# Retrieval step of an encoder layer: picks of two heads side by side, rank keys in pairs, two one-hot parts on ScalarE, 40 side rows for 48, new tables

## The reference

```python
q = (h @ wq).reshape(nb, L, 8, 256)
s1 = einsum(q[..., :128], keys1); s2 = einsum(q[..., 128:], keys2)   # 128 scores each
v1, i1 = top_k(s1, 16);  v2, i2 = top_k(s2, 16)
cand = v1[..., :, None] + v2[..., None, :]                          # 256 sums
sc, ci = top_k(cand, 16)
e = i1[ci // 16] * 128 + i2[ci % 16]                                # expert's number
w = softmax(sc)
act = gelu(einsum('td,tjd->tj', h, u_tab[e]))                       # 128 experts a token
y = einsum('tj,tjd->td', w * act, v_tab[e])
```

## Time and profile before

| what | value |
|---|---|
| median of 3 runs | 3218.49 us (3216.95 to 3223.83) |
| the profiled execution | 3227.11 us, its span 3225.4 us |
| PE, DVE, POOL, ACT busy | 91%, 73%, 38%, 22% of the span |
| bytes moved | 919.78 MB, of which gathers 536.94 MB |
| step 6, from its tile 2 to the last row | 1117.7 to 3160 us of the span |

### The profile page before, as it was taken

The page is one execution under the profiler, slowest core; times in us unless marked ns, Lnnn a source line. Parts: engine busy times, 40 slices in busy tenths (PEclk is TensorE's granted clock), DMA queues, the critical chain, the costliest instruction groups (busy, mean ns, idle before and its releaser), DMA issues. The chain is left out here.

```text
span 3225.4 us, 31301 instructions
## 1 busy us (share of the span) xinstructions
PE 2929.4 (91%) x10332; PEld 1580.0 (49%) x10332; DVE 2348.0 (73%) x4427; ACT 701.4 (22%) x1179; POOL 1222.1 (38%) x1101
## 2 busy tenths in 40 slices
PE   6999699779689997899999998997799999999995
PEld 2557477667574443444544553443344444444442
DVE  4696545550688699999999998774766666676775
ACT  3111434321221101343452442342000000000003
POOL 0111111021225545334334335553655444455660
PEclk8998899889889998999999999998899999999997
DMA  4441101023238999899899899999999999999994
GB/s 181 174 163 47 59 27 33 27 79 124 78 98 346 413 387 341 307 327 372 320 334 354 307 348 379 385 415 405 390 405 404 404 404 404 404 403 404 397 395 162
DMA packets 285835, 919.78 MB, mean 285 GB/s; under 512 B 25840, under 2 KB 75248, under 8 KB 278256
## 3 DMA queue, kind: packets, MB, share of 16 engines
q0 software_dynamic: 147456, 536.94, 43.2%
q1 hardware_dynamic: 99584, 301.75, 25.0%
q10 hardware_dynamic: 38640, 79.18, 6.5%
HBM read 830.21 MB, written 87.56 MB: 285 GB/s over the span
## 5 line engine op out<-in xcount | busy, mean ns | idle before, releaser
L1519 PE MATMUL s_pu<-s_hn,s_ut 128*128 128x512 f32 x2304 | 1016.6, 597 | 14.5 <-ACT s_gst L1631 8.0
L1474 POOL DMA_INDIRECT s_slot<-in_u,s_row x512 | 513.9, 1004 | 688.7 <-DVE s_slot L1888 570.8
L1901 DVE SCALAR_TENSOR_TENSOR s_hB<-s_slot,s_dot,s_hB 128x1024 f32<-128x1024 f32 x461 | 585.1, 1284 | 259.8 <-DMA s_slot<-in_v,s_row 225.6
L1474 POOL DMA_INDIRECT s_slot<-in_v,s_row x512 | 561.7, 1097 | 454.8 <-DVE s_hB L1901 369.6
L1519 PEld LDWEIGHTS s_pu<-s_hn,s_ut 128*128 128x128 f32 x2304 | 436.9, 192 | 546.8 <-issue 546.8
L1888 DVE SCALAR_TENSOR_TENSOR s_slot<-s_slot,s_ph 128x1024 f32<-128x1024 f32 x512 | 608.5, 1220 | 64.9 <-DMA s_slot<-in_u,s_row 40.5
L302 PE MATMUL s_ps<-hn_hi,w_hi 128*128 128x512 f32 x704 | 289.1, 411 | 81.9 <-PEq L276 40.7
L1605 PE MATMUL s_pw<-s_ct,s_vt 128*128 128x512 f32 x512 | 243.3, 598 | 45.4 <-DVE s_ct L1909 42.3
L303 PE MATMUL s_ps<-hn_lo,w_hi 128*128 128x512 f32 x704 | 280.6, 399 | 0.0
L1605 PE MATMUL s_pu<-s_ct,s_vt 128*128 128x512 f32 x512 | 242.6, 596 | 0.0
L1605 PE MATMUL s_py<-s_ct,s_vt 128*128 128x512 f32 x512 | 240.6, 592 | 0.0
(11 more groups left out here) (284 smaller groups left out, 3006.6 us busy)
## 6 DMA issues: line engine op xcount, KB each, us to landing
s_ut<-in_u_tiles SPq DMA_DIRECT2D x128, 512.0 KB
s_vt<-in_v_tiles SPq DMA_DIRECT2D x32, 2048.0 KB
s_g<-s_gst ACTq DMA_DIRECT2D x128, 256.0 KB
s_w<-s_wb ACTq DMA_DIRECT2D x16, 2048.0 KB
s_gr<-s_g SPq DMA_DIRECT2D x64, 512.0 KB
s_wr<-s_w SPq DMA_DIRECT2D x16, 2048.0 KB, 35.0
s_ada<-in_ada SPq DMA_DIRECT2D x48, 512.0 KB, 5.3
s_ada<-in_ada SPq DMA_DIRECT2D x4, 2048.0 KB, 24.6
```

The lines of the kernel that those rows point to most:

```text
L1474: pool.indirect_dma_start(out=slot[s][:, :], out_offset=None, in_=io[kind], in_offset=bass.IndirectOffsetOnAxis(ap=row[b][:, j:j + 1], axi ...
L1519: mm = pe.matmul(pu[:, n % 2, :], ut[n % UR][:, k, :], hn[:, k, :], start=(k == 0), stop=(k == DC - 1))
L1901: dve.scalar_tensor_tensor(y, s, dot[b][:, j:j + 1], y, ALU.mult, ALU.add).then_inc(taken, 1)
```

## The change

- Picks: `pick_step` does two heads side by side in 6 steps, each followed by one drain or two, in place of 3 parts a head. There are still 24 steps to a ranking. In step 5 the two lanes are the two blocks.
- `ranked_key`: the array `eq` has the pairs innermost (`[16, 64, 2]` walked in twos, the keys doubled), and the sum over 16 is four adds that halve it in place of one reduction.
- One-hot parts: VectorE makes one part, ScalarE two (16 activations a batch; they and `later_ready` take the place of the third part and its semaphore).
- `SIDE_ROWS` 48 becomes 40, over 74 tiles in place of 98, so that the last is at tile 98. `take_y` moves to tile 100.
- Tables: `RANKED`, `RANK_TILES` 16 to 17, `HOT_AT` and `HOT_TILES`, `sparse_by`; the order of v rows (`wanted`): six rounds without block 3 first, and each v row waits for the row before it of the same block.

```diff
-                for i in range(MADE_PICKS):
-                    for part in range(3):
-                        m.picks[i].part(dve, h, part, sc[:, :, RANKED[i], :])
+                for step in range(PICK_STEPS):
+                    pick_step(dve, [(m.picks[i], h, 0, sc[:, :, RANKED[i], :]) for i in range(MADE_PICKS)], step)
...
+def pick_step(dve, lanes, step):
+
+    if step == 0:
+        for pk, h, v, sc in lanes:
+            for n in range(2):
+                dve.max(out=pk.val[:, 2 * h + n, 0:8], in_=sc[:, n, :])
...
+    elif step == 4:
+        for pk, h, v, sc in lanes:
+            dve.max(out=pk.best[:, h, 0:8], in_=pk.cand[v][:, :])
         dve.drain()
...
-RANKED = (0, 1, 4, 5, 2, 6, 3, 7)
+RANKED = (0, 1, 4, 2, 5, 6, 3, 7)
...
-SIDE_ROWS = 48
+SIDE_ROWS = 40
...
+V_LEAD = 6
 SPARSE_OPS = 2 * SPARSE * P - SIDE_ROWS
-RANK_AT, RANK_TILES = 2, 16
-HOT_AT = (21, 47, 73, 101)
-HOT_TILES = 22
-SIDE_AT, SIDE_TILES = 26, 98
+RANK_AT, RANK_TILES = 2, 17
+HOT_AT, HOT_TILES = (24, 55, 80, 106), (26, 22, 22, 16)
+SIDE_AT, SIDE_TILES = 26, 74
...
-        tenths += (45 if t < RANK_AT else 44 if t < HOT_AT[0] else
-                   29 if t < RANK_AT + RANK_TILES * (len(RANKED) - MADE_PICKS) else 48 if t < 123 else 60)
+        tenths += 45 if t < RANK_AT else 42 if t < 22 else 32 if t < 104 else 43 if t < 123 else 50
...
-            def third_parts(a, r):
+            def later_parts(a, r):
...
-                for i in range(8):
-                    q, t = divmod(i, 2)
-                    o = act.activation(hotw[n % 2][2][:, q, :, t], hot1[n % 2][:, q, :, t], ACT.Copy,
-                                       scale=rest[:, 1, 8 * r + i:8 * r + i + 1])
-                o.then_inc(third_ready, 1)
+                for x in range(2):
+                    for i in range(8):
+                        q, t = divmod(i, 2)
+                        o = act.activation(hotw[n % 2][1 + x][:, q, :, t], hot1[n % 2][:, q, :, t], ACT.Copy,
+                                           scale=rest[:, x, 8 * r + i:8 * r + i + 1])
+                o.then_inc(later_ready, 1)
...
-            take_y()
+                if n == side_tile(SIDE_ROWS - 1) + 2:
+                    take_y()
...
-                    dve.tensor_tensor(eq[:, :, :], halff[s][:, :].unsqueeze(2).broadcast_to([P, P, TOPK]),
-                                      count[:, :].unsqueeze(1).broadcast_to([P, P, TOPK]), ALU.is_equal)
+                    dve.tensor_tensor(eq[:, :, :].rearrange("p a (q t) -> p a q t", t=2),
+                                      halff[s][:, :].rearrange("p (q t) -> p q t", t=2).unsqueeze(1).broadcast_to(shape),
+                                      count[:, :, :].unsqueeze(2).broadcast_to(shape), ALU.is_equal)
...
-                    dve.tensor_reduce(pair_of(i)[:, s, :], eq[:, :, :], AX.X, ALU.add)
+                    for n in (8, 4, 2):
+                        dve.tensor_tensor(eq[:, 0:n, :], eq[:, 0:n, :], eq[:, n:2 * n, :], ALU.add)
+                        dve.drain()
+                    dve.tensor_tensor(pair_of(i)[:, s, :], eq[:, 0, :], eq[:, 1, :], ALU.add)
...
-                for x in range(2):
-                    dve.tensor_tensor(hotw[n % 2][x][:, :, :, :], hot1[n % 2][:, :, :, :], spread(wT[x]), ALU.mult)
+                dve.tensor_tensor(hotw[n % 2][0][:, :, :, :], hot1[n % 2][:, :, :, :], spread(wT[0]), ALU.mult)
...
-                    dve.wait_ge(taken, i - 2)
+                    if j > (0 if b else SIDE_ROWS):
+                        dve.wait_ge(taken, number["v", b, j - 1] + 1)
```

More of the change, by code:

```diff
@@ L1205, in __init__ @@
         self.place = buffer("place", [P, PH, TOPK], U32)
[L1207 to L1214, removed]
+PICK_STEPS = 6
+def pick_step(dve, lanes, step):
[3 more added lines that the diff above has]
+                dve.max(out=pk.val[:, 2 * h + n, 0:8], in_=sc[:, n, :])
+    elif step == 1:
+        for pk, h, v, sc in lanes:
+            for n in range(2):
+                best = pk.val[:, 2 * h + n, 0:8]
+                dve.max_index(pk.key[:, 2 * h + n, 0:8], best, sc[:, n, :])
+                dve.match_replace(out=pk.rep[v][n][:, :], in_to_replace=best, in_values=sc[:, n, :], imm_value=LOWEST)
+    elif step == 2:
+        for pk, h, v, sc in lanes:
+            for n in range(2):
+                dve.max(out=pk.val[:, 2 * h + n, 8:16], in_=pk.rep[v][n][:, :])
+    elif step == 3:
+        for pk, h, v, sc in lanes:
+            for n in range(2):
+                dve.max_index(pk.key[:, 2 * h + n, 8:16], pk.val[:, 2 * h + n, 8:16], pk.rep[v][n][:, :])
+            at = 0
+            for a0, a1, nb in CAND_RANGES:
+                na = a1 - a0
+                dve.tensor_tensor(pk.cand[v][:, at:at + na * nb].rearrange("p (a b) -> p a b", a=na),
+                                  pk.val[:, 2 * h, a0:a1].unsqueeze(2).broadcast_to([P, na, nb]),
+                                  pk.val[:, 2 * h + 1, 0:nb].unsqueeze(1).broadcast_to([P, na, nb]), ALU.add)
+                at += na * nb
+    elif step == 4:
+        for pk, h, v, sc in lanes:
+            dve.max(out=pk.best[:, h, 0:8], in_=pk.cand[v][:, :])
@@ L1215, in best8 @@
         dve.drain()
-        for n in (2 * h, 2 * h + 1):
-            dve.max_index(self.key[:, n, 0:8], self.val[:, n, 0:8], sc[:, n % 2, :])
-            dve.match_replace(out=self.rep[n % 2][:, :], in_to_replace=self.val[:, n, 0:8], in_values=sc[:, n % 2, :],
+        for pk, h, v, sc in lanes:
+            dve.max_index(pk.place[:, h, 0:8], pk.best[:, h, 0:8], pk.cand[v][:, :])
+            dve.match_replace(out=pk.cand2[v][:, :], in_to_replace=pk.best[:, h, 0:8], in_values=pk.cand[v][:, :],
@@ L1219, in best8 @@
                               imm_value=LOWEST)
+    else:
+        for pk, h, v, sc in lanes:
+            dve.max(out=pk.best[:, h, 8:16], in_=pk.cand2[v][:, :])
         dve.drain()
[L1222 to L1249, removed]
+        for pk, h, v, sc in lanes:
+            dve.max_index(pk.place[:, h, 8:16], pk.best[:, h, 8:16], pk.cand2[v][:, :])
@@ L1824, in ranking @@
                         dve.wait_ge(sc_in[i % 2], 16 * ((i - MADE_PICKS) // 2 + 1))
-                    m.picks[i % MADE_PICKS].part(dve, x // 3, x % 3, sc[i % 2][:, x // 3 * 2:x // 3 * 2 + 2, :])
+                    pair, step = divmod(x, PICK_STEPS)
+                    pick_step(dve, [(m.picks[i % MADE_PICKS], h, h % 2, sc[i % 2][:, 2 * h:2 * h + 2, :])
+                                    for h in (2 * pair, 2 * pair + 1)], step)
                 elif x == 24:
@@ L1850, in take_picks @@
                 dve.drain()
+                dve.tensor_copy(rest[:, 0, :], wT[1][:, :])
+                dve.drain()
             def one_hots(a, r):
@@ L2039, in encoder_layer @@
     m.head = head_inputs(m)
-    m.picks = [Picks(m, R0 + 104 * KB + 4608 * s, s) for s in range(MADE_PICKS)]
+    m.picks = [Picks(m, R0 + 104 * KB + 6144 * s, s) for s in range(MADE_PICKS)]
     m.h1_back = m.at("h1_back", [P, DC, T], F32, F0)
```

49 lines of the change are left out of this document (29 added, 20 removed).

## The result

The changed kernel takes 3166.1 us (median of 4 runs, 3162.1 to 3173.8) where the kernel before takes 3218.0 in runs beside it: ratio 0.9838, 95% interval 0.9815 to 0.9861. A second set of runs gave 0.9845 (0.9829 to 0.9862). The forecast was 3177, range 3152 to 3207, faster. The profiled execution took 3162.1 us, its span is 3160.4.

What follows compares the result with a forecast made beforehand. TensorE was taken to bound tiles 27 to 97, transfers everything from tile 98. Terms -23.1 + 2.8 + 5 - 30 + 5 - 1.3 = -41.6 from 3227.1 give 3185.5, less 8.6 for the median: 3177 us, range 3152 to 3207.

Steps and rivals of the forecast that it cites:

- Tile 27: Step 6, start of tile 27: VectorE's shorter work lets TensorE start it at 1313.9, not 1337.0: -23.1 us.
- Tiles 27 to 97: Step 6's middle stretch: TensorE sets the pace, 628.2 us for 625.4, plus 5 for late side rows.
- +2.8: Tiles 27 to 97: two batches fewer and three side rows more on TensorE cost 2.8 us.
- +5: Tiles 27 to 97: side rows that land late, with the gathers' share at 360 GB/s, cost 5 us.
- From tile 98 on: Tile 98 to the last row: transfers bound, 467.2 MB left at 400 GB/s, -30 us, and +5 for tiles 98 to 103.
- The copy of py: `take_y` at tile 100 removes a 32.97 us VectorE stall, priced at nothing because transfers ran at 400 GB/s.
- Step 5, -1.3: Step 5: the last head's picks of two blocks save 8 drains, -1.3 us.
- What would show it: Signs in step 6's trace, among them tile 27 near 1314, tile 98 near 1947, VectorE's v-phase lead used up.
- The stretch's limit: Rival: transfers in tiles 27 to 97 are already at their limit, 337 GB/s; +28 us, 3205; chance 0.14.
- TensorE alone: Rival: TensorE is the bound after tile 98 too, gathers filling every gap; -91 us, 3127; chance 0.04.
- ScalarE: Rival: ScalarE's activations, above 0.37 us each, hold TensorE in each batch's tile; +90 us, 3267; chance 0.05.
- Nothing: Rival: the change changes nothing, as transfers set all of step 6 and its bytes are the same; chance 0.04.

Runs made afterwards that it cites:

- e3: The changed kernel with the copy of py (`take_y`) put back behind the last gelu: 3166.9 us, ratio 0.9800 to the kernel before.
- e5: The changed kernel with gathered v rows from the start of the v phase on fetched at half width: 3138.1 us, ratio 0.9740 to the kernel before.
- e12: The changed kernel with u rows 81 to 174 fetched at half width: 3169.8 us, ratio 0.9803 to the kernel before.
- e1: The changed kernel's new instructions under the tables of the kernel before, with 48 side rows: 3192.7 us, ratio 0.9881 to the kernel before.
- e2: The instructions of the kernel before under the changed kernel's tables, 40 side rows and v-row order: 3200.5 us, ratio 0.9910 to the kernel before.
- e8: The changed kernel with a ranking over 16 tiles; 3.8 rows a tile to tile 23, 3.5 to 81, 3.7 to 103: 3143.2 us, ratio 0.9761.
- e13: The changed kernel with a ranking over 16 tiles; 3.2 rows a tile to tile 23, 3.7 to 103: 3138.6 us, ratio 0.9715.
- e4: The changed kernel with two one-hot parts made by VectorE and one by ScalarE: 3173.9 us, ratio 0.9831 to the kernel before.
- e14: The changed kernel with a ranking over 16 tiles; 3.5 rows a tile to tile 23, 3.7 to 103: 3138.6 us, ratio 0.9711.
- e15: The changed kernel with step 6's picks made one head after the other again: 3184.0 us, ratio 0.9843 to the kernel before.
- e9: The changed kernel with a ranking over 16 tiles; 4.2 rows a tile kept to tile 21, then 3.5 to 103: 3145.6 us, ratio 0.9764.
- e11: The changed kernel measured again, nothing changed: 3170.0 us, ratio 0.9845 to the kernel before.

## Why the prediction came out as it did

**Right in sign and range, 11 us too high.** The likeliest case is the one that happened, but the nearness of the number is in part luck. Between the two spans lie 65.0 us where the sum had 41.6. Two terms of it were off in opposite directions, tile 27 by +9.5 and the stretch to tile 98 by -17.5; and 15.2 us more lie ahead of the ranking and behind the last row, which the sum had at nothing. The medians are only 51.8 apart, because the profiled execution of before was 9.1 us above its median and that of the changed kernel 4.0 below.

**Tile 27, mis-sized.** The sum had the ranking at 49.0 and 93 rows (90, and three in tile 24), the first one-hot 174.3 us behind the ranking's start and tile 27 another 8.7 behind that: 183.0, and so -23.1. Its two traces have 192.5 and 192.6 (e3 and e5, the same kernel up to there, 192.9 and 192.6), so -13.6. The prices of single instructions were right (1222, 690, 426 ns; 4.81 us of ScalarE for 4.9). The 9.5 us are these:

- 7.5 us ahead of the first one-hot, which comes at 181.8. A quicker VectorE asks for rows that have not landed: where none is late, in e12, it comes at 176.2, so that is 5.6 us. The last 1.9 are VectorE's own, and no run takes them apart.
- 2.0 us behind it, 10.7 for 8.7. TensorE had stood idle for 20.39 us, and its 24 matmuls took 2.5 us start to start and the side row 2.6, where the sum had 1.4 and 1.8. The granted clock in these 5 us was 0.59 of full speed, so most of them ran at 1.2 and not at 2.4 GHz:

```profile
1306.28:1311.37 5.09, 5.09 (x28) 3.68 (x29) 4.94 (x14) 1.84 (x7) 2.10 (x3) 0.59 0.79 249
```

The rows had it: the earlier trace rows show 2.72 us for the 24 matmuls right behind a wait, and 1.37 only later; the sum took the second. The step that failed took VectorE alone as the bound of a window in which the DMA engines were busy 94% of the time before and 99% after.

**Tiles 27 to 97, wrong in sign: -9.7 and not +7.8.** The step that failed is its starting point. It took 625.4 us as TensorE's own pace because TensorE was busy 98.6% of it. Its pieces, by the prediction's own durations, are 71 x 6.87 + 45 x 1.37 + 35 x 1.82 = 613.1, so 12 us of the 625.4 were not its own. Of these the profile shows 8.8 as idle time, 7.0 of them for side rows. The same sum for the new tables is 71 x 6.87 + 43 x 1.37 + 38 x 1.82 = 615.9; four traces measured 615.6 to 615.8, two more 616.5 and 616.7. The +2.8 for batches and side rows was thus right as a difference of pieces. The +5 for late side rows was the wrong way round: they were late before and aren't now, which fits a VectorE with slack (544 us busy for 586; see e1 and e2).

**From tile 98 on, as forecast.** 467.7 MB were left (forecast 467.2), they moved at 398.4 GB/s (400), the last row came 1173.9 us behind tile 98 (1173). The end behind the last row is 6.0 us shorter. Before, the last row ended 5.9 us ahead of the start of TensorE's last matmul; now it ends 0.2 ahead of it. So the old v phase, 880.7 us, was TensorE's 128 x 6.87 = 879, with 3.1 us of waits for v tiles and the transfers close behind (400 GB/s there too), and not bound by them as the first part of the prediction said. In the changed kernel it is theirs: 906.0 us, 17.7 of waits for v tiles, and e5 takes them away.

**The copy of py, priced at nothing: right** by the traces of e3. **Step 5, -1.3:** TensorE's wait at the start of step 6 went from 11.35 us to 9.98, -1.4.

**What would show it.** The turned picks' wait is gone, the middle ran at 361 GB/s, and VectorE's lead shrinks in the v phase and TensorE waits there, as foretold. But the lead isn't used up, 5 us of it are left at the least; the waits are for v tiles and not for VectorE. Tile 27 at 1311.4 looks like a hit for 1314, and isn't: the ranking started 12 us earlier and the way from it was 9.5 us longer than forecast. Tile 98 came at 1927.1, not 1947, for the same reason and that of the middle. The v phase starts 29 us behind the last u tile and not within 15: VectorE has v rows ahead of its first product and they land late, so this start too hangs on transfers. Timeline of VectorE at the phase's start:

```profile
2182.26 1.28 DVE L1919 SCALAR_TENSOR_TENSOR s_hB<-s_slot,s_dot,s_hB 128x1024 f32<-128x1024 f32 x1 [0.39 <-DMA s_slot<-in_v,s_row]
2187.32 1.28 DVE L1919 SCALAR_TENSOR_TENSOR s_hB<-s_slot,s_dot,s_hB 128x1024 f32<-128x1024 f32 x1 [3.77 <-DMA s_slot<-in_v,s_row]
...
2193.47 0.75 DVE L1915 TENSOR_SCALAR s_hB<-s_slot,s_dot 128x1024 f32<-128x1024 f32 x1 [4.67 <-DMA s_slot<-in_v,s_row]
2194.14 2.49 DVE L1927 TENSOR_TENSOR s_ct<-s_gr,s_wr 128x512 f32<-128x512 f32 x4
```

**The rivals.** The stretch's limit: out, by 375 and 381 GB/s in e8 and e13, as by 391 in the changed kernel's first window; the Trainium skill's 358 GB/s (page "DMA: Bandwidth & Descriptors", section "Where 436 GB/s comes from") is passed in every window of the changed kernel's step 6. TensorE alone: not in the changed kernel, but 411 GB/s from tile 98 to 123 in e8 is nearer to its 425 than the forecast thought possible. ScalarE: out, 0.30 us an activation. Nothing: out.

**The 9.2 us ahead of the ranking** go with a pause that comes and goes with the execution, with the old code and with the new: see the last section.

## What to carry to other kernels

Work out an engine's own pace in a stretch from its pieces, however busy it looks: at 98.6% busy, 12 us of the stretch were not TensorE's own, and most of them were waits for a queue that went with how busy another engine was. Price the first instructions behind a long wait from rows that also stand behind one. Where an engine is made quicker in a window whose transfers are at 94% or more, count only on what the rows' landing lets through. The gain is had in stretches that have both engine and transfer slack, and moving bytes there (3.7 rows a tile for 3.2 in the middle) was worth as much again as half of the change. And take a transition's time from a local distance (ranking to tile 27), not from its absolute time in one execution.

## What the runs showed of the hardware

**A pause that comes and goes.** Between 993 and 1018 us TensorE goes through its tiles evenly in some executions and pauses in others, with no wait that the profile shows. From tile -16 to tile 2 the kernel before, e2, e4, e12, e14 and e15 take 149 to 155 us, e1 and e13 141 and 146, the changed kernel, its second trace, e3, e5, e8 and e9 139.6. e12, then the second trace of the changed kernel, timeline of TensorE:

```profile
993.57 3.17 PE L1526 MATMUL s_pu<-s_hn,s_ut 128*128 128x512 f32 x7
1005.40 2.08 PE L1536 MATMUL s_pw<-keysT,s_gst 128*128 128x128 f32 x8 [8.66 <-issue]
```

```profile
994.71 7.03 PE L1525 MATMUL s_pu<-s_hn,s_ut 128*128 128x512 f32 x16
1001.58 1.05 PE L1535 MATMUL s_pw<-keysT,s_gst 128*128 128x128 f32 x8
```

The kernels of one chip (e12 to e15) all have it, e13 a short one, and those of another (e5, e8, e9, e11) none; of the third (e1 to e4), e2 and e4 have it, e1 hardly and e3 not. In the kernel before tile -12 takes 17.5 us for 7.76; that makes the 9.2 us of the table. What it is stays open, and so is whether it follows the chip, since each kernel has one trace only (the changed one two, on two chips).

**Transfer rates.** With v rows, u tiles and the table `w` together, 411 GB/s held for 201 us in e8 (412 in e13), above the 400 that the v phase shows in every kernel with full rows.
